# Two far value tiles of the first attention, computed with the activations as the stationary operand

## The reference, cut to what matters

```
qkv = (x @ w_qkv).reshape(B, S, N_DIL_GROUPS, 3, N_HEADS, HEAD_DIM)
for g, (window, dil) in enumerate(DIL_CONFIGS):     # ((128, 1), (512, 4), (2048, 16))
    o, l = _dilated_group(qkv[:, :, g, 0], qkv[:, :, g, 1], qkv[:, :, g, 2],
                          window, dil, slopes[g])
    outs.append(o)
    lses.append(l)
wts = jax.nn.softmax(jnp.stack(lses), axis=0)
o = jnp.sum(wts[..., None] * jnp.stack(outs), axis=0)
return o.reshape(B, S, ATTN_WIDTH).astype(x.dtype) @ w_out
```

## Time and profile before

| | |
|---|---|
| median of 3 runs | 3410.52 us (3409.12 to 3412.01) |
| the profiled execution | 3411.94 us, of it 3410.1 us span |
| granted TensorE clock, mean | 0.997 of full speed |
| PE, PEld busy | 99%, 92% of the span |
| DVE, ACT, POOL busy | 74%, 51%, 4% of the span |

### The profile page before, as it was taken

One profiled execution on the slowest core, in us unless ns is written; L12 is line 12 of the kernel. 1 busy time (PEld: TensorE's weight loads), 2 busy tenths in 40 slices (PEclk: granted clock), 3 DMA queues, 4 the chain that ended last, 5 costly groups with the idle time before them and its releaser, 6 DMA issues. The chain is left out here.

```text
span 3410.1 us, 65717 instructions
## 1 busy us (share of the span) xinstructions
PE 3367.1 (99%) x25107; PEld 3146.1 (92%) x25107; DVE 2521.6 (74%) x3720; ACT 1726.3 (51%) x2640; POOL 136.2 (4%) x130
## 2 busy tenths in 40 slices
PE   9999999999999999999999999999999999999998
PEld 8998899989998989898899889999999998799987
DVE  6886888887888778787888865557785367777863
ACT  4563655545554545454545545446555344555552
POOL 0100202000200100000001000000000000000000
PEclk9999999999999999999999999999999999999999
DMA  4333223332333322222233321211223321123332
GB/s 141 111 102 113 88 88 104 111 111 94 99 105 111 107 75 87 75 87 87 69 106 106 116 93 63 75 62 64 99 98 99 94 75 43 39 75 100 98 99 81
DMA packets 89676, 311.33 MB, mean 91 GB/s; under 512 B 10816, under 2 KB 15296, under 8 KB 89472
## 3 DMA queue, kind: packets, MB, share of 16 engines
q1 hardware_dynamic: 89056, 307.19, 27.7%
q0 software_dynamic: 416, 1.29, 0.1%
HBM read 306.34 MB, written 2.10 MB: 90 GB/s over the span
## 5 line engine op out<-in xcount | busy, mean ns | idle before, releaser
L872 PE MATMUL ps<-x_hi,w_hi 128*128 128x264 f32 (+2 forms) x1840 | 572.8, 311 | 2.6 <-ACT pair L2844 0.9
L872 PE MATMUL ps<-x_hi,w_lo 128*128 128x264 f32 (+2 forms) x1840 | 562.9, 306 | 0.0
L872 PE MATMUL ps<-x_lo,w_hi 128*128 128x264 f32 (+2 forms) x1840 | 561.9, 305 | 0.0
L872 PE MATMUL ps<-h_hi,w_hi 128*128 128x264 f32 (+3 forms) x1282 | 406.7, 317 | 4.3 <-DVE h_lo L3160 1.9
L872 PE MATMUL ps<-h_hi,w_lo 128*128 128x264 f32 (+3 forms) x1282 | 395.9, 309 | 0.0
L872 PE MATMUL ps<-h_lo,w_hi 128*128 128x264 f32 (+3 forms) x1282 | 395.1, 308 | 0.0
L872 PEld LDWEIGHTS ps<-x_hi,w_hi 128*128 128x128 f32 x1840 | 347.1, 189 | 32.0 <-issue 10.2
L872 PEld LDWEIGHTS ps<-x_hi,w_lo 128*128 128x128 f32 x1840 | 347.8, 189 | 14.7
L872 PEld LDWEIGHTS ps<-x_lo,w_hi 128*128 128x128 f32 x1840 | 346.3, 188 | 15.8
L2953 DVE TENSOR_TENSOR w_lo<-raw,w_hi 128x1024 fp32r<-128x1024 f32 x214 | 260.9, 1231 | 109.8 <-ACT w_hi L1808 105.8
L967 PE MATMUL ps<-t_hi,w_hi 128*128 128x256 f32 x1152 | 322.7, 280 | 0.0
(11 more groups left out here) (417 smaller groups left out, 8829.0 us busy)
## 6 DMA issues: line engine op xcount, KB each, us to landing
raw<-wstream SPq DMA_DIRECT2D x577, 512.0 KB, 3.3
res<-xT SPq DMA_DIRECT2D x8, 256.0 KB, 7.4
out<-res SPq DMA_DIRECT2D x8, 256.0 KB, 2.2
near_bias<-consts POOLq DMA_DIRECT2D x1, 512.0 KB, 3.9
g_chunk<-consts POOLq DMA_DIRECT2D x1, 264.0 KB, 3.1
g_keep<-consts POOLq DMA_DIRECT2D x1, 256.0 KB, 3.2
par<-params SPq DMA_DIRECT2D x1, 232.5 KB, 7.3
far_bias<-consts POOLq DMA_DIRECT2D x1, 128.0 KB, 2.6
```

Of the source, the lines that this page charges most:

```text
L872: m = pe.matmul(ps[:, bank, 0:n], w[:, slot, wt, :], x[:, k, c0:c0 + n], start=first and q == 0, stop=last and q == 2)
```

## The change

In pairs 1 to 7 the two far value tiles are no longer computed as tiles and turned. `value_rows` computes them turned: for each residue r the activations of its 128 tokens are the stationary operand, every fourth column of `x_hi` or `x_lo` (a step of 4 fp32 elements), and the weight tiles of j = 7 and 8, 128 columns each in two slots, move together, 256 columns. The result, 128 tokens by 256 channels, goes to bank 0 or 1 in turn, and ACT stores it to `val` in one instruction for a residue (`store_rows`). Two `take`, two `store` and the two `turn_values` of these tiles go. Where the second tile's slot is the lower one, the two tiles are stored in `val` in reverse order, and `weigh` picks them by `value_place`. Pair 0 and the near tile stay as they were.

```diff
+        def value_slots(st, p):
+
+            a, b = attend_slot(st, p, 7), attend_slot(st, p, 8)
+            return slice(a, b + 1) if a < b else slice(b, a + 1, a - b)
@@ weigh
                     if not near:
                         pe.wait_ge(A["val"], 3 * p + 3)
+                        pe.wait_ge(s_evac, st["t0"] + 9 * p + 9)
@@ second_part
                     if t == 3:
                         turn_maxima(p)
-                        turn_values(p, 2)
+                        if not p:
+                            turn_values(p, 2)
@@ attend1 on PE
+                def value_rows(p):
+
+                    t, slots = st["t0"] + 9 * p, value_slots(st, p)
+                    pe.wait_ge(s_lo, st["u0"] + 9 * p + 9)
+                    for r in range(R4):
+                        if r < 2:
+                            pe.wait_ge(s_evac, t + 6 + r)
+                        else:
+                            pe.wait_ge(A["val"], 3 * p + 1 if r == 2 else 3 * p + 3)
+                        for k in range(KD):
+                            hi, lo = (x[:, k, META:T].rearrange("p (i r) -> p r i", r=R4)[:, r, :] for x in x_src)
+                            for n, (x, w) in enumerate(((hi, w_hi), (hi, w_lo), (lo, w_hi))):
+                                m = pe.matmul(ps[:, r % 2, 0:2 * P], x, w[:, slots, k, :],
+                                              start=k == 0 and n == 0, stop=k == KD - 1 and n == 2)
+                            if k == KD - 1:
+                                if r < R4 - 1:
+                                    m.then_inc(A["vtr"], 1)
+                                else:
+                                    m.then_inc(s_unit, 2)
+                            if (r, k) == (0, 5):
+                                turn_values(p, 0)
+                                scores(p, 2)
+                                scores(p, 3)
...
-                    for j in range(6, 9):
-                        unit_of(p, j)
+                    unit_of(p, 6)
+                    value_rows(p)
@@ attend1 on ACT
+                def store_rows(p, r):
+
+                    if r < R4 - 1:
+                        act.wait_ge(A["vtr"], turned(p) + r + 2)
+                    else:
+                        act.wait_ge(s_unit, st["u0"] + 9 * p + 9)
+                    act.wait_ge(A["pv"], p)
+                    act.activation(val[:, r, 1:3, :], ps[:, r % 2, 0:2 * P].rearrange("p (g n) -> p g n", g=2), ACT.Copy)\
+                        .then_inc(A["val"] if r < 2 else s_evac, 1)
...
                 for p in range(1, KD):
+                    snap(p, 0, 1)
                     high(p, 0, 3)
-                    snap(p, 0, 1)
                     high(p, 1, 0)
                     snap(p, 0, 3)
-                    store(p - 1, 2)
+                    if p == 1:
+                        store(0, 2)
...
                         high(p + 1, 0, 1)
+                        store_rows(p, 0)
                         store(p, 0)
-                        take(p, 7)
+                        for r in range(1, R4):
+                            store_rows(p, r)
                         high(p + 1, 0, 2)
-                        store(p, 1)
-                        take(p, 8)
                         continue
```

More of the change, by code:

```diff
@@ L672, in attend_slot, with turned, value_place @@
             return (st["u0"] + 3 + 15 * (p - 1) + (step if j < 6 else j - 6)) % RING
+        def turned(p):
+            return 3 + 4 * (p - 1) if p else 0
+        def value_slots(st, p):
+            a, b = attend_slot(st, p, 7), attend_slot(st, p, 8)
+            return slice(a, b + 1) if a < b else slice(b, a + 1, a - b)
+        def value_place(st, p, g):
+            return 3 - g if g and p and attend_slot(st, p, 7) > attend_slot(st, p, 8) else g
         def attend_pack(p, g):
@@ L1396, in weigh @@
                             for r in range(R4):
-                                both(lambda out: out[:, r * P:(r + 1) * P], lambda half: val[:, r, g, head(half)],
+                                both(lambda out: out[:, r * P:(r + 1) * P], lambda half: val[:, r, value_place(st, p, g), head(half)],
                                      lambda half: scored[:, half, g - 1, r * P:(r + 1) * P], (g, r) == (1, 0), False)
@@ L2216, in take @@
                         v = 3 * p + j - 6
-                        if v >= 2:
+                        if p >= 2:
+                            act.wait_ge(A["vtr"], turned(p - 1) + 1)
+                        elif v >= 2:
                             act.wait_ge(A["vtr"], v - 1)
@@ L2273, in store @@
                 def store(p, g):
-                    v = 3 * p + g
-                    act.wait_ge(A["vtr"], v + 1)
+                    act.wait_ge(A["vtr"], turned(p) + g + 1)
                     if p >= 1:
@@ L2381, in attend1 @@
                     split(nxt + 1, (nxt + 1) % RING)
-                    store(p, 0)
                     for k in range(3, 6):
                         att_high(k)
-                    take(p, 7)
+                    store_rows(p, 0)
+                    store(p, 0)
+                    store_rows(p, 1)
                     att_high(6)
-                    store(p, 1)
-                    take(p, 8)
-                store(KD - 1, 2)
+                    store_rows(p, 2)
+                    store_rows(p, 3)
                 weights(KD - 1, False)
```

## The result

| | us, median (runs) | ratio to before, 95% interval |
|---|---|---|
| before | 3410.55 (4) | |
| changed | 3483.72 (4) | 1.0213 (1.0201 to 1.0225) |

The change costs 73.2 us. The forecast was 3476 us, the likeliest case's own range 3463 to 3490, and the whole range, drawn down to the free load, 3406 to 3490.

A forecast was written before the change was run, and what follows sets the result against it. PE was taken to bound the kernel, busy 99% of the span. The exchange's -3.9 us and the stepped loads' +69.7 us, with waits at nothing, gave +66 us on 3410.5: 3476 us, range 3406 to 3490.

The forecast's parts named there:

- likeliest case: Far value tiles: the stepped weight load sets PE's pace, 3476 us, own range 3463 to 3490, chance 0.70.
- free load: Rival at the far value tiles: the stepped load is no dearer, 0.112 us, giving 3406.6 us; chance 0.16.
- PE is the bound, a microsecond there is one of the kernel: Far value tiles, pairs 1 to 7: PE busy 13.94 of 13.94 us, so its changes there count in full.
- The exchange with the places left aside: Far value tiles: 256-column products for 512-column ones, +2.4 us; 14 transpose groups gone, -6.3 us; together -3.9 us.
- The load of the stepped operand sets the pace: 672 new products: each load takes 0.223 us in place of 0.1193 us a product, +69.7 us.
- The price from writes of other engines: Stepped load of the new products: priced from DVE's and ACT's stepped writes at 0.207 or 0.240 us, middle 0.223.
- So four neighbouring elements seem to cost one access, and stepped ones one access each, on both engines: Support for the load's price, from PE's moving reads and DVE's `normalise`: 128 accesses of 1.75 ns, 0.224 us.
- The rule of the Trainium skill: New products' loads: each column is a new 16-byte line, so all 672 pay; another sentence could mean -3.9 us.
- The waits at nothing: Four places around the far value tiles that could be late, all reckoned covered; 0.3 us left before `widen`.
- E: The time at which a pair's value tiles end, 1270.69 before the change; DVE's later work was reckoned from it.
- the rival of a late DVE: Pack behind the value tiles: DVE late, 0.7 us a pair, 3412 us with a load at no cost; chance 0.05.
- The signs: Profile after: new products' starts 0.21 to 0.24 us apart, far-tile stretch from 13.94 to about 23.5 us.

The follow-up runs named there:

- step-1 kernel: The changed kernel with the new products' stationary operand taken as 128 neighbouring columns, not every fourth: 3405.24 us, 0.9983 of the kernel before.
- step 8: The changed kernel with the new products' stationary operand read from a slot of weights, every eighth fp32 column: 3486.77 us, 1.0222 of the kernel before.
- kernel with moving step 4: The kernel of before with tiles 7 and 8 of pairs 1 to 7 taking moving activations every fourth column, so ACT's take needn't sort: 3486.62 us, 1.0222.

## Why the prediction was right, by its own steps

- **PE is the bound, a microsecond there is one of the kernel.** Shown: 10.45 us a pair in the windows of pair 1, 73.1 us for seven, 73.2 measured.
- **The exchange with the places left aside, -3.9 us.** The step-1 kernel is this term by itself: 0.9983 (0.9974 to 0.9992), 6.1 us less, of which the interval leaves 2.7 to 8.9. Its period of a pair is 57.79 us (first starts of L1482 at 1256.73 and 1314.52) against 58.52, so -5.1 us for seven. The 256-column products go at 0.118 there and not 0.1193 us, 672 x 0.001 = 0.9 us of the difference.
- **The load of the stepped operand sets the pace, +69.7 us.** The mechanism is shown: the pace follows the step (1, 2, 3, 4), with everything else in the instruction stream the same, step 8 hardly adds to step 4, and at step 4 the pace doesn't change with 128, 256 or 512 moving columns. The size was somewhat low: 0.2356 us a load and not 0.223, so 672 x (0.2356 - 0.1193) = 78.2 us. The spans of the changed and of the step-1 kernel differ by 3482.6 - 3404.3 = 78.3 us, and 78.3 - 5.1 is the 73.2 measured. The forecast of +66 was 7 us too low: the load's term by 8.5 us, of which the exchange gave 1.2 back.
- **The price from writes of other engines.** The bound from ACT's stepped write, 0.240 us, came near the measured 0.2356, nearer than the middle of the two bounds. That is an agreement of numbers, and in part luck: no run ties DVE's and ACT's writes to PE's read.
- **"So four neighbouring elements seem to cost one access, and stepped ones one access each, on both engines".** This step failed in part. For the load's stepped columns it holds: 64, 96, 128 and 128 touched groups for steps 2, 3, 4 and 8, at about 1.84 ns each, give 0.118 (hidden), 0.177 (0.174 measured), 0.236 and 0.236 us (0.242). For its side-by-side columns it doesn't: 32 groups would take 0.059 us, and such a load takes 0.112, so something else sets the pace there. And it was argued from the pace of the moving operand, 1.75 ns for four columns, and that likeness didn't bear out: the moving side takes 0.90 ns for a stepped element, half an access, and nearly as much, 0.89, with a step of 2.
- **The rule of the Trainium skill.** The Trainium skill's page "SBUF — State Buffer", section "Specifications (TRN2)", asks for at least two hits on a line of 16 bytes for full bandwidth. For the load the runs agree with it: a step of 2 (two hits) costs next to nothing, a step of 3 pays and a step of 4 more. The other sentence, in the section "Door 1: The DMA port swizzle (why `[64,N]` ≈ `[32,N]`)" of that page of the Trainium skill, read as making a step of 4 fp32 free, is not borne out: 0.2356 against 0.118 us. On the moving side a step of 2 paid nearly in full (0.453 against 0.2316 us), against the first rule.
- **The waits at nothing.** `high` of step 2 ended at 1283.17, E + 1.5 (E = 1281.64), E + 1.7 was reckoned. `tops` ended 2.28 us ahead of `widen` before (1276.87 and 1279.15), and 0.15 us ahead of it in the changed kernel (1289.51 and 1289.66); in the step-1 kernel it is 0.12 us in pair 1:

```profile
1277.00 1.28 DVE L3709 TENSOR_REDUCE top_q<-ps 128x4 f32<-128x512 f32 x2
```

```profile
1278.40 1.03 PE L1393 MATMUL ps<-ident,top_q 128*128 128x128 f32 x8
```

  They end at 1278.28, and PE gets there at 1278.40; 0.3 us had been reckoned. In both kernels the only waits of `widen` for DVE are in pair 0, at 1220.4 and 1220.5, ahead of the first changed product, and they were there before too. So the rival of a late DVE was close, but stayed out.
- **The signs.** The starts lie 0.2356 us apart, inside the 0.21 to 0.24 forecast. The stretch of the far tiles was to be "about 23.5 us"; the terms given for it add up to 23.8, and it is 24.83, the rest being the load's low price.

**No version that beats both was found.** The step-1 kernel shows what one would gain, 3 to 9 us, but it is not the reference's computation. It would need the activations of this stage sorted by residue in a buffer of their own, 2 x 8 x 512 x 4 bytes = 32 KB a partition, and by the kernel's list of buffers the stage has no room for that. Sorting `x_hi` and `x_lo` in place behind pair 0 would need the packs, the near tile and the copies to `qk` rewritten; it wasn't tried, nor was a layout with 512 moving columns beside each stepped load, which needs the far tiles of two pairs in the four slots at once.

## What to carry to other kernels

Before exchanging the operands of a matmul, ask how each is laid out in its new place: here a stationary operand of fp32 with a step of 4 elements loads in 0.236 us where neighbouring columns take 0.112, and with 256 moving columns there was only 0.007 us of cover over the latter. A step of 2 was nearly free in that place, and 512 moving columns all but hide the step of 4; a step in the moving operand had no such cover and halved the pace with 2 and with 4. If the product must come out sorted, let an engine with idle time do the sorting: ACT's sorting copy takes 1.11 us and took 0.60 in the kernel with moving step 4, where it doesn't sort, and PE, busy for 13.94 of 13.94 us there, didn't wait for it.

## What the runs showed of the hardware that was not expected

- The moving side and the load have different rules for a step: 0.89 and 0.90 ns an element for steps of 2 and 4 (0.45 side by side), against about 1.84 ns for each touched group of four on the load. At step 4 both take about twice their side-by-side time; at step 2 only the moving side does.
- The stepped load's pace hardly changed with TensorE's granted clock: 0.236 us at 0.50, 0.234 at 1.00.
- A stretch in which PE never idles can lose the clock: with 128 columns moving every 0.23 us it fell to 0.50, with 256 columns every 0.236 us it stayed at 1.00. That cost 20 us over seven pairs, in the work around those products.
